# A hybrid decoder layer: sums of squares as two rounded products, and three engines' orders rewritten in the mixer loop

## The chip, the cores and the metric

The program runs on one core of one Trainium2 chip. The metric is the device time of one execution in microseconds (us); lower is better.

## The reference, cut to what matters

One decoder layer for 512 tokens of width 1024. The first half (the mixer) projects the normalised input onto eight heads of differential attention and eight groups of a Mamba-2 scan; the second half is a mixture of 32 experts, which the change leaves alone. What the change touches is the normalisation of queries and keys, and of the attention output:

```python
def _rms_norm(x, g, eps):
    xf = x.astype(jnp.float32)
    y = xf * lax.rsqrt(jnp.mean(xf * xf, axis=-1, keepdims=True) + eps)
    return (y * g.astype(jnp.float32)).astype(x.dtype)
...
    q = _rms_norm(q.reshape(b, s, ATTN_HEADS, 2, ATTN_HEAD_DIM), q_g, RMS_EPS) * (ATTN_HEAD_DIM ** -0.5)
    k = _rms_norm(k.reshape(b, s, ATTN_HEADS, 2, ATTN_HEAD_DIM), k_g, RMS_EPS)
...
    o = _rms_norm(o, sub_g, RMS_EPS) * (1.0 - lambda_init)
```

Around it in the same step of the kernel run the scan (decay, `mix`, state, `y`), the softmax of the scores, and the projections of the next step.

## The kernel before

The mixer is a loop of eight steps, one per attention head and scan group (`steps_of_mixer`; the eighth is written out after the loop). Every engine has a body of its own, and the order of the calls in it is the order of its instructions. The engines meet only at semaphores: `x_ready.at(i, n)` is the n-th signal of step i.

All projections use a split: a float32 matrix is rounded to fp32r (`hi`), the rest is kept as `lo`, and three products hi*hi, hi*lo, lo*hi stand for one float32 product. ScalarE (ACT) rounds a 512 KB weight piece in its `split(i, p)`, VectorE (DVE) subtracts in its own `split(i, p)`, and SyncE (SP) loads the next piece when VectorE is done. A step has nine pieces: 0 to 5 for projections 0 to 5 (`project(i, n)`), 6 to 8 for `project_vz`. Those of step i+1, 0 to 5, are split during step i.

TensorE (PE) goes through a step like this: `project(i, 4)` (queries), `turn_xb(0)` and `cb(0)`, `project(i, 5)` (keys), `turn_xb(1)`, `sum_squares(0)`, `y_and_state(0)`, `turn_xb(2)`, `project_vz(0)`, `sum_squares(1)`, `turn_xb(3)`, `cb(1)`, `project_vz(1)`, `scores(0)`, `y_and_state(1)`, and then, between quarters and halves of the next step's projections 0 to 3, three more scores and states, four `turn_diff`, the product with the values (L1443), `turn_y`, and the sum of squares of the attention output (L1451, osum below). `sum_squares(n)` waits for ScalarE's `squares(n)`, and is one float32 matmul with a block matrix of ones:

```python
pe.matmul(s_b[n][:], block_ones, sq[:, n], start=True, stop=True).then_inc(sums_ready.sem, 1)
```

Its result goes to ScalarE's `root(n)` (Ln, then Exp), then to VectorE's `norm_qk(n)` (L1063), and `scores(0)` waits for both. The result of osum goes through a Ln and an Exp on ScalarE (L928, L929) to VectorE's scaling of the attention output (L1197), behind which stand `split(i+1, 5)` and, in the next step, `taps(i+1, 3)` (L991), ScalarE's `silu(3)`, its table load, `make_decay(0)` (L822), `squares(0)` (L792, L793), `take_xb(0)` (L817), and the splits of pieces 7 and 8 (L711).

`y_and_state(1)` on TensorE waits for `make_mix(1)` of VectorE and for `make_xs(1)` of GpSimd (POOL). GpSimd has two jobs: `make_seg(u)` (L648, L651: two 128x512 operations on cumulative sums that SP brings by a DMA of its own) and `make_xs(u)` (L662 twice, L665: three 128x256 operations). Its order is seg 0, seg 1, xs 0, seg 2, xs 1, seg 3, xs 2, xs 3. SP brings the rows of seg 2 behind weight piece 2 and those of seg 3 behind piece 3, and such a piece waits for VectorE's split of the piece three before it:

```python
sp.wait_ge(plo_ready.sem, plo_ready.at(i + 1, p - MRAW + 1))
```

So the rows of seg 2 wait for VectorE's `split(i, 8)` (L985, `vz_lo`), those of seg 3 for its `split(i+1, 0)`.

VectorE's gated output (`gate_y(0)`, L1136) starts ScalarE's `norm_y(0)` (L845), behind which stands ScalarE's `split(i+1, 1)`, and behind that VectorE's. The logits are made at L1082, their negated maximum at L1087, and the difference of the softmaxes at L1100 to L1103.

Of the kernel before, what the change touches and what calls it, by code (L numbers as in the profile page):

```python
# [16 lines left out]
P = 128  # L17
D = 1024
# [214 lines left out]
def decoder_layer(nc, x, small, consts, onehot_rows, gffn, rel_bias, par, w_mix, w_dt, w_tail, w_rt, w1, w2, b12,  # L233
                  tok_ids, pads, out):
    with ExitStack() as ctx:
# [3 lines left out]
        def sem(name):  # L239
            return ctx.enter_context(nc.semaphore(name))  # L240
# [86 lines left out]
        def parts(name, shape, base, at):  # L327
# [12 lines left out]
        seg_of = (aux[:, 3 * T:4 * T].rearrange("p (k n) -> p k n", k=2), dT[:, 2:4, 0:2 * P])  # L340
        wm_hi = [parts(f"wm_hi{n}", [P, KT, P], base, at) for n, (base, at) in enumerate(spots)]
# [69 lines left out]
        ovhot_ready, ovhot_used, ovtable_ready, over_ready = (sem("ovhot_ready"), sem("ovhot_used"),  # L411
                                                              sem("ovtable_ready"), sem("over_ready"))

# [122 lines left out]
        with nc.Block() as block:  # L536
# [96 lines left out]
            @block.gpsimd  # L633
            def _(pool):
                prime(pool, seg_ready, xs_ready, gidx_ready, sidx_ready, pickb_ready, picks_ready, *spare_used[0:2])
                pool.wait_ge(decays_ready, 3)
                with pool.Fori(0, HEADS) as i:
                    h4 = i * HPG

                    def heads(table, u):  # L640
                        return table[:, u, bass.ds(h4, HPG)]

                    def make_seg(u):

                        pool.wait_ge(rows_in[u % 2].sem, rows_in[u % 2].at(i, u // 2 + 1))
                        of = seg_of[u % 2].rearrange("p k (h c) -> p k h c", h=2)
                        at = heads(a_all, u).rearrange("p (k h) -> p k h", k=2)
                        pool.tensor_tensor(of, of, at.unsqueeze(3).to_broadcast([P, 2, 2, P]), ALU.subtract).then_inc(  # L648
                            seg_ready.sem, 1)
                        pool.wait_ge(seg_ready.sem, seg_ready.at(i, 2 * u + 1))  # L650
                        pool.tensor_tensor(of, of, tri.unsqueeze(1).unsqueeze(1).to_broadcast([P, 2, 2, P]), ALU.mult).then_inc(  # L651
                            seg_ready.sem, 1)

                    def make_xs(u):

                        pool.wait_ge(m0_read.sem, m0_read.at(i, u + 1))
                        pool.wait_ge(m1_ready.sem, m1_ready.at(i, min(2 * u, 6)))
                        pool.wait_ge(ydiag_ready.sem, ydiag_ready.at(i, u))
                        pool.wait_ge(y_read.sem, y_read.at(i, u))
                        xv = xb[:, u, 0:GW].rearrange("p (h c) -> p h c", h=HPG)  # L660
                        for dst, src in ((xdt, heads(dtv, u)), (xw, heads(wend, u))):
                            pool.tensor_tensor(dst.rearrange("p (h c) -> p h c", h=HPG), xv,  # L662
                                               bcast_inner(src, HD), ALU.mult)
                        dsk = SMALL["d_skip"][0]
                        pool.tensor_tensor(xd.rearrange("p (h c) -> p h c", h=HPG), xv,  # L665
                                           bcast_inner(smalls[:, bass.ds(h4 + dsk, HPG)], HD),
                                           ALU.mult).then_inc(xs_ready.sem, 1)

                    make_seg(0)
                    for u in range(NT):  # L670
                        if u < NT - 1:
                            make_seg(u + 1)
                        make_xs(u)

            @block.scalar
            def _(act):
                prime(act, sigz_ready, phi_ready, ghi_ready, sigm_ready, mhi_ready, taps_ready, silu_ready, proj_read, root_ready, m0_read, decay_ready, exp_ready, yn_ready,
# [102 lines left out]
                def body(i, more):  # L780
# [99 lines left out]
                    make_decay(1)  # L880
# [21 lines left out]
                    softmax_exp(3)  # L902
                    norm_y(2, 0)
                    if more:
                        tap(i + 1, 1)
                        take_y(0, 7)
                        split(i + 1, 4)
                    else:
                        take_y(0, 7)
# [27 lines left out]
            def _(dve):  # L937
# [116 lines left out]
                def body(i, more):  # L1054
# [83 lines left out]
                    taps(i, 3)  # L1138
                    split(i, 6)
                    masked_cb(0)  # L1140
# [67 lines left out]
            def _(pe):  # L1208
# [115 lines left out]
                def body(i, more):  # L1324
                    def project_vz(t):
                        free_proj(i, 6 + t)
                        pe.wait_ge(plo_ready.sem, plo_ready.at(i, PIECES))
                        hi, lo = (w[:].rearrange("p (a b) -> p a b", a=KT) for w in (vz_hi, vz_lo))
                        for k in range(KT):
# [4 lines left out]
                        ins.then_inc(proj_done.sem, 1)  # L1334
# [340 lines left out]
            def _(pe):  # L1675
# [427 lines left out]
                def head_ov():  # L2103
                    pe.wait_ge(part_ready, NADD)
                    pe.wait_ge(first_added.sem, first_added.at(2))
                    for t in range(NT):
                        pe.wait_ge(ovhot_ready, t + 1)
# [3 lines left out]
                        ins.then_inc(ovhot_used if t < NT - 1 else ovtable_ready, 1)  # L2111
# [234 lines left out]
            def _(dve):  # L2346
# [369 lines left out]
                def head_ov():  # L2716
# [37 lines left out]
                    for t in range(NT):  # L2754
                        n = slice(TOPK * t, TOPK * (t + 1))
                        if t:
                            dve.wait_ge(ovhot_used, t)
# [4 lines left out]
                            ovhot_ready, 1)  # L2762
# [263 lines left out]
```

## Time and profile before

| | us |
|---|---|
| median of 3 runs | 1873.24 (1871.5 to 1873.26) |
| the profiled execution, its own time | 1872.48 |
| span of the profiled execution | 1870.4 |
| TensorE busy | 1831.9 |
| VectorE, ScalarE, GpSimd busy | 1128.1, 943.0, 359.9 |

The mixer loop runs from about 50 us to 590 us of the span, a step in 68.7 us. A row of the timeline has its start and its duration in us, engine, line, operation, output and inputs with shapes, and how many instructions were merged into it (x2, x3); in brackets stands the idle time of the engine before it, and what ended it. A float32 matmul is recorded as two rows of its line; the start of the next operation shows how long the engine was taken. Durations of matmuls overlap: in a stream, the distance of the starts is the price.

### The profile page before, as it was taken

The page shows a single profiled execution, that of the slowest core. Times are in us where ns is not written, and L with a number is a line of the kernel's source. Part 1 is how long each engine was busy: PE and PEld are TensorE (multiplying, and loading weights), DVE is VectorE, ACT ScalarE, POOL GpSimd, SP SyncE. Part 2 cuts the span into 40 slices and gives each one's busy share as a digit, 9 for nine tenths or more (in the row PEclk, how much of TensorE's full clock was granted, in tenths as well). Part 3 has the DMA queues.
Part 4 walks back from the last instruction along what each step waited for, and adds up shares of the span by engine and source line. Part 5 has one row for each costly group of instructions (what it writes and reads, how often), then busy time and mean ns, then how long its engine had stood idle before and what let it go on. Part 6 is the DMA issues. An engine that isn't in the chain of part 4 may idle for free.

```text
span 1870.4 us, 27360 instructions
## 1 busy us (share of the span) xinstructions
PE 1831.9 (98%) x8657; PEld 1298.2 (69%) x8657; DVE 1128.1 (60%) x1371; ACT 943.0 (50%) x1312; POOL 359.9 (19%) x401
## 2 busy tenths in 40 slices
PE   8999999999999999999999999999999999999998
PEld 6887887887888888887655665566556655665563
DVE  7767867867867333448654565456545654565456
ACT  5676676666667222325454455445544554455441
POOL 1322332332330000013111112111211121112010
PEclk9999999999999999999999999999999999999999
DMA  6232232232241222458999999999999999999998
GB/s 203 86 123 93 82 132 93 76 129 101 81 138 57 93 99 97 154 196 323 418 419 421 422 422 421 422 421 421 421 421 421 421 421 422 421 422 420 422 419 347
DMA packets 95377, 520.06 MB, mean 278 GB/s; under 512 B 13522, under 2 KB 20858, under 8 KB 45032
## 3 DMA queue, kind: packets, MB, share of 16 engines
q1 hardware_dynamic: 87672, 501.08, 67.3%
q0 software_dynamic: 6944, 16.30, 2.3%
q10 hardware_dynamic: 720, 2.16, 0.3%
q8 instruction: 22, 0.36, 0.1%
q14 instruction: 19, 0.16, 0.0%
HBM read 511.52 MB, written 25.51 MB: 287 GB/s over the span
## 4 chain that ended last, share of the span: by engine, by line
PE 81%; DMA 11%; DVE 4%; issue 2%; ACT 1%; SPq 0%; DVEq 0%; ACTq 0%
PE bank L1929 18%; PE bank L1301 15%; PE bank L1687 10%; DMA big<-in_w 10%; PE bank L1960 7%; PE bank L1331 7%; PE bank L1969 6%; PE bank L1952 2%; DVE w_lo L2535 2%; PE bank L1376 2%; PE bank L1359 1%; PE bank L1872 1%; DVE x_lo L2547 1%; PE bank L1443 1%; DMA keep<-in_b 1%
## 5 line engine op out<-in xcount | busy, mean ns | idle before, releaser
L2535 DVE TENSOR_TENSOR w_lo<-big,w_hi 128x2048 fp32r<-128x2048 f32 x141 | 321.7, 2291 | 205.3 <-ACT w_hi L2222 205.3
L2222 ACT ACTIVATE w_hi<-big 128x2048 fp32r<-128x2048 f32 x141 | 268.8, 1918 | 230.7 <-DMA big<-in_w 206.5
L1960 PE MATMUL bank<-big,keep 128*64 128x512 f32 x896 | 203.3, 598 | 0.0
L2535 DVE TENSOR_TENSOR w_lo<-keep,w_hi 128x2048 fp32r<-128x2048 f32 x48 | 109.9, 2292 | 103.4 <-ACT w_hi L2222 102.8
L1301 PE MATMUL bank<-h_hi,wm_hi 128*128 128x512 f32 x408 | 168.6, 413 | 0.0
L1301 PE MATMUL bank<-h_hi,wm_lo 128*128 128x512 f32 x408 | 159.5, 391 | 0.0
L1301 PE MATMUL bank<-h_lo,wm_hi 128*128 128x512 f32 x408 | 159.1, 390 | 0.0
L2222 ACT ACTIVATE w_hi<-keep 128x2048 fp32r<-128x2048 f32 x48 | 92.2, 1921 | 105.7 <-DMA keep<-in_w 96.1
L1960 PEld LDWEIGHTS bank<-big,keep 128*64 128x64 f32 x896 | 59.9, 136 | 117.3 <-issue 117.2
L1929 PE MATMUL bank<-w_hi,x_hi 128*128 128x512 f32 x480 | 134.4, 402 | 3.7 <-DVE w_lo L2535 3.7
L1929 PE MATMUL bank<-w_lo,x_hi 128*128 128x512 f32 x480 | 128.9, 390 | 0.0
L1929 PE MATMUL bank<-w_hi,x_lo 128*128 128x512 f32 x480 | 128.7, 390 | 0.0
L1929 PEld LDWEIGHTS bank<-w_hi,x_hi 128*128 128x128 f32 x480 | 86.6, 188 | 50.6 <-issue 21.8
L2356 DVE TENSOR_TENSOR g_lo<-keep,g_hi 128x1024 fp32r<-128x1024 f32 x35 | 42.9, 1225 | 113.0 <-ACT g_hi L2147 113.0
L1929 PEld LDWEIGHTS bank<-w_lo,x_hi 128*128 128x128 f32 x480 | 90.1, 188 | 19.6
L1929 PEld LDWEIGHTS bank<-w_hi,x_lo 128*128 128x128 f32 x480 | 90.1, 188 | 19.3
L1952 PE MATMUL bank<-w_hi,a_hi 128*128 128x512 f32 x256 | 84.5, 411 | 19.1 <-DVE w_lo L2535 19.1
L1301 PEld LDWEIGHTS bank<-h_hi,wm_hi 128*128 128x128 f32 x408 | 76.7, 188 | 26.2 <-issue 12.3
L991 DVE SCALAR_TENSOR_TENSOR big<-bank,par_sb,big 128x511 f32<-128x511 f32 (+2 forms) x96 | 71.8, 748 | 29.4 <-ACT big L732 20.7
L1331 PE MATMUL bank<-vz_hi,h_hi 128*128 128x384 f32 x256 | 89.2, 348 | 0.0
L1301 PEld LDWEIGHTS bank<-h_hi,wm_lo 128*128 128x128 f32 x408 | 76.6, 188 | 16.5
L1301 PEld LDWEIGHTS bank<-h_lo,wm_hi 128*128 128x128 f32 x408 | 76.8, 188 | 15.9 <-issue 1.9
(401 smaller groups left out, 3628.3 us busy)
## 6 DMA issues: line engine op xcount, KB each, us to landing
big<-in_w SPq DMA_DIRECT2D x290, 1024.0 KB, 13.4
keep<-in_w SPq DMA_DIRECT2D x94, 1024.0 KB, 14.1
big<-in_w_mix SPq DMA_DIRECT2D x72, 512.0 KB, 3.3
keep<-in_w_tail SPq DMA_DIRECT2D x44, 512.0 KB, 3.3
keep<-in_x SPq DMA_DIRECT2D x8, 512.0 KB, 4.8
aux<-acum_rows SPq DMA_DIRECT2D x16, 256.0 KB, 3.8
big<-acum_rows SPq DMA_DIRECT2D x16, 256.0 KB, 3.6
keep<-y_tok SPq DMA_DIRECT2D x4, 1024.0 KB, 13.2
```

The costliest lines, as they stand in the source:

```text
L991: ins = dve.scalar_tensor_tensor(out=conv[:, n, s:T], in0=proj_b[n % 2][:, 0:T - s], scalar=w, in1=conv[:, n, s:T], op0=ALU.mult, op1=ALU.add)
L1301: ins = pe.matmul(to[:], w[:, k], h[:, k], start=(k == 0 and w is hi and h is h_hi), stop=(k == KT - 1 and w is lo))
L1331: ins = pe.matmul(proj_b[t % 2][:, 0:VZ], h[:, k, t * P:(t + 1) * P], w[:, k], start=(k == 0 and h is h_hi and w is hi), stop=(k == KT - 1 ...
L1376: ins = pe.matmul(y_b[:, h * HD:(h + 1) * HD], mix[:, h], xdt[:, h * HD:(h + 1) * HD], start=True, stop=True)
L1687: ins = pe.matmul(bank[to][:], w[:, k], v[:, (x or 0) + k], start=(start and k == 0 and w is hi and v is x_hi_), stop=(stop and k == KT - ...
L1929: ins = pe.matmul(bank[c][:], x_part, w_part[:, s, c * 512:(c + 1) * 512], start=False, stop=n == KT - 1 and w_part is w_hi and x_part is lo)
L1952: ins = pe.matmul(bank[4 + c][:], a_part, w_part[:, s, o:o + 512], start=False, stop=k == KT - 1 and w_part is w_hi and a_part is lo)
L1960: ins = pe.matmul(bank[2 * (c // 2)][r, :], x_s[:, n % 4, CS * (n // 4):CS * (n // 4 + 1)], raw[s][:, c * 512:(c + 1) * 512], start=False, ...
L1969: ins = pe.matmul(bank[4][CS * c:CS * (c + 1), :], a_s[:, k % 4, CS * (k // 4):CS * (k // 4 + 1)], raw[s][:, o:o + 512], start=False, stop ...
L2222: act.activation(w_hi[:, s], raw[r], ACT.Copy).then_inc(hi_ready, 1)
L2356: dve.tensor_tensor(lo, of, hi.bitcast(F32), ALU.subtract).then_inc(glo_ready.sem, 1)
L2535: dve.tensor_tensor(w_lo[:, s], raw[r], w_hi[:, s].bitcast(F32), ALU.subtract).then_inc(lo_ready, 1)
```

## The change

- `sum_squares(n)` and osum are no longer one float32 matmul but two fp32r matmuls into one bank: ones times `sq_hi`, ones times `sq_lo`. The ones are rounded once before the loop (two copies on GpSimd).
- ScalarE gets three copies 128x512 a step (`high_square(0)`, `high_square(1)`, and one for osum), which round `sq` to `sq_hi`; GpSimd gets three subtractions 128x512 (`low_square`), which make `sq_lo`. TensorE waits for them. On GpSimd two stand between `make_xs(0)` and `make_seg(2)`, the third at the step's end; `make_seg` of the next step's first block moves ahead of the third.
- TensorE: `project_vz(0)` is cut in three. A quarter goes ahead of `y_and_state(0)`; `sum_squares(0)` moves behind five eighths of it. Each part waits only for the pieces that it reads. osum moves a quarter of `project(i+1, 3)` later.
- VectorE: `masked_cb(0)` ahead of `split(i, 6)`; `next_state(0)` and `sum_y(0)` ahead of `norm_qk(0)`; `split(i+1, 0)` behind `masked_cb(1)` and `make_mix(1)`; `norm_qk(1)` ahead of `silu_z(0)`.
- ScalarE: `silu(3)` and the table load ahead of `split(i, 6)`; `make_decay(1)` ahead of `root(0)`; `take_y(0, 7)` ahead of `norm_y(2, 0)`.
- Two semaphores of a later stage are shared with older ones; no instruction goes with it.

```diff
 (GpSimd)
+                def low_square(i, n, at):
+                    pool.wait_ge(sqhi_ready.sem, sqhi_ready.at(i, at))
+                    pool.tensor_tensor(sq_lo[:, n], sq[:, n], sq_hi[:, n].bitcast(F32), ALU.subtract).then_inc(
+                        sqlo_ready.sem, 1)
+                def body(i, more):
+                    make_seg(i, 1)
+                    make_xs(i, 0)
+                    low_square(i, 0, 1)
+                    low_square(i, 1, 2)
+                    make_seg(i, 2)
+                    make_xs(i, 1)
+                    make_seg(i, 3)
+                    make_xs(i, 2)
+                    make_xs(i, 3)
+                    if more:
+                        make_seg(i + 1, 0)
+                    low_square(i, 0, 3)
 (ScalarE)
+                    def high_square(n):
+                        act.wait_ge(proj_read.sem, proj_read.at(i, n + 1))
+                        act.wait_ge(diff_ready.sem, diff_ready.at(i, 0))
+                        act.activation(sq_hi[:, n], sq[:, n], ACT.Copy).then_inc(sqhi_ready.sem, 1)
                     silu(2)
-                    split(i, 6)
                     silu(3)
                     act.preload_act_table_set("natural_log_exp_and_others")
+                    split(i, 6)
                     make_decay(0)
                     squares(0)
                     take_xb(0)
+                    high_square(0)
                     split(i, 7)
                     split(i, 8)
                     squares(1)
                     take_xb(1)
+                    high_square(1)
                     take_xb(2)
+                    make_decay(1)
                     root(0)
-                    make_decay(1)
                     split(i + 1, 0)
...
                     act.activation(sq[:, 0], m1_b[:], ACT.Square).then_inc(osq_ready.sem, 1)
+                    act.wait_ge(osq_ready.sem, osq_ready.at(i, 1))
+                    act.activation(sq_hi[:, 0], sq[:, 0], ACT.Copy).then_inc(sqhi_ready.sem, 1)
 (VectorE)
                     taps(i, 3)
+                    masked_cb(0)
                     split(i, 6)
-                    masked_cb(0)
                     make_mix(0)
                     split(i, 7)
                     split(i, 8)
-                    norm_qk(0)
                     next_state(0)
                     sum_y(0)
-                    split(i + 1, 0)
+                    norm_qk(0)
                     masked_cb(1)
                     make_mix(1)
+                    split(i + 1, 0)
+                    norm_qk(1)
                     silu_z(0)
-                    norm_qk(1)
                     gate_y(0)
                     logits(0)
 (TensorE)
-                        pe.matmul(s_b[n][:], block_ones, sq[:, n], start=True, stop=True).then_inc(sums_ready.sem, 1)
+                        pe.wait_ge(sqlo_ready.sem, sqlo_ready.at(i, n + 1))
+                        pe.matmul(s_b[n][:], block_r[:], sq_hi[:, n], start=True, stop=False)
+                        pe.matmul(s_b[n][:], block_r[:], sq_lo[:, n], start=False, stop=True).then_inc(
+                            sums_ready.sem, 1)
...
                     turn_xb(1)
-                    sum_squares(0)
+                    project_vz(0, 0, KT // 4)
                     y_and_state(0)
                     turn_xb(2)
-                    project_vz(0)
+                    project_vz(0, KT // 4, 5 * KT // 8)
+                    sum_squares(0)
+                    project_vz(0, 5 * KT // 8, KT)
                     sum_squares(1)
...
                     turn_y(2, 8)
+                    project(i + 1, 3, KT // 2, 3 * KT // 4)
                     pe.wait_ge(osq_ready.sem, osq_ready.at(i, 1))
                     pe.wait_ge(logits_ready.sem, logits_ready.at(i, 4))
-                    pe.matmul(s_b[0][:], ones, sq[:, 0], start=True, stop=True).then_inc(osum_ready.sem, 1)
-                    project(i + 1, 3, KT // 2, KT)
+                    pe.wait_ge(sqlo_ready.sem, sqlo_ready.at(i, 3))
+                    pe.matmul(s_b[0][:], ones_r[:].to_broadcast([P, P]), sq_hi[:, 0], start=True, stop=False)
+                    pe.matmul(s_b[0][:], ones_r[:].to_broadcast([P, P]), sq_lo[:, 0], start=False, stop=True).then_inc(
+                        osum_ready.sem, 1)
+                    project(i + 1, 3, 3 * KT // 4, KT)
```

## Rows read from the trace of the kernel before

**Rows 1.** The page's busy line of TensorE.

```profile
PE 1831.9 (98%) x8657; PEld 1298.2 (69%) x8657; DVE 1128.1 (60%) x1371; ACT 943.0 (50%) x1312; POOL 359.9 (19%) x401
```

**Rows 2.** Waits of TensorE, 30 to 640 us: total, times, longest.

```profile
PEld bank L1301 <- issue: 14.2, 32, 0.8
...
PEld bank L1393 <- ACT keep L860: 1.6, 7, 0.2
```

**Rows 3.** Timeline of TensorE, third step of the mixer.

```profile
190.79 1.02 PE L1349 MATMUL bank<-keep,cst 128*128 128x512 f32 x2
...
197.50 1.02 PE L1349 MATMUL bank<-keep,cst 128*128 128x512 f32 x2
198.36 0.49 PE L1341 MATMUL bank<-cst,big 128*128 128x128 f32 x3
...
203.19 0.49 PE L1359 MATMUL bank<-big 64*128 64x128 f32 x4
203.61 1.10 PE L1376 MATMUL bank<-keep 128*128 128x64 f32 x8
...
214.96 0.92 PE L1359 MATMUL bank<-big 64*128 64x384 f32 x4
...
223.67 0.49 PE L1393 MATMUL bank<-cst,aux 128*128 128x128 f32 x3
...
243.79 1.02 PE L1451 MATMUL bank<-keep,cst 128*128 128x512 f32 x2
...
244.88 0.39 PE L1301 MATMUL bank<-h_lo,wm_hi 128*128 128x512 f32 x1
245.11 0.39 PE L1301 MATMUL bank<-h_hi,wm_lo 128*128 128x512 f32 x1
```

**Rows 4.** The same engine, `scores(0)` one step on.

```profile
271.86 0.49 PE L1359 MATMUL bank<-big 64*128 64x128 f32 x4
```

**Rows 5.** Timeline of GpSimd, third step.

```profile
189.49 1.60 POOL L665 TENSOR_TENSOR keep<-big,smalls 128x256 f32<-128x256 f32 x1
197.00 1.96 POOL L648 TENSOR_TENSOR aux<-aux,a_all 128x512 f32<-128x512 f32 x1 [5.91 <-DMA aux<-acum_rows]
...
202.07 1.06 POOL L665 TENSOR_TENSOR keep<-big,smalls 128x256 f32<-128x256 f32 x1
...
204.39 1.28 POOL L651 TENSOR_TENSOR big<-big,cst 128x512 f32<-128x512 f32 x1
```

**Rows 6.** Timeline of VectorE, third step.

```profile
180.23 2.54 DVE L991 SCALAR_TENSOR_TENSOR big<-bank,par_sb,big 128x511 f32<-128x511 f32 x3 [0.65 <-ACT big L732]
...
188.95 3.22 DVE L985 TENSOR_TENSOR vz_lo<-big,vz_hi 128x1024 fp32r<-128x1024 f32 x2 [1.76 <-ACT vz_hi L711]
...
202.58 0.83 DVE L1136 TENSOR_TENSOR big<-big 128x256 f32<-128x256 f32 x1
...
204.87 0.83 DVE L1087 TENSOR_SCALAR st<-st 128x2 f32<-128x2 f32 x1
206.12 1.23 DVE L985 TENSOR_TENSOR wm_lo<-big,wm_hi 128x1024 fp32r<-128x1024 f32 x1 [0.42 <-ACT wm_hi L718]
...
213.44 0.74 DVE L1082 TENSOR_TENSOR aux<-bank,biasT 128x256 f32<-128x256 f32 x2
...
222.56 0.62 DVE L1103 SCALAR_TENSOR_TENSOR aux<-aux,st 128x384 f32<-128x384 f32 x1
```

**Rows 7.** Timeline of ScalarE, third step.

```profile
186.37 0.58 ACT L792 ACTIVATE big<-bank 128x512 f32<-128x512 f32 x1
...
187.85 2.01 ACT L711 ACTIVATE vz_hi<-big 128x1024 fp32r<-128x1024 f32 x2
...
193.89 0.68 ACT L797 ACTIVATE keep<-bank,eps 128x512 f32<-128x512 f32 x1
...
203.53 0.42 ACT L845 ACTIVATE yn<-big 128x256 f32<-128x256 f32 x1 [2.40 <-DVE big L1136]
```

**Rows 8.** Timeline of the DMA queue: the rows of seg 2 are issued.

```profile
192.96 0.33 SPq L597 DMA_DIRECT2D aux<-acum_rows  x1
```

More of the change, by code:

```diff
@@ L340, in decoder_layer @@
         seg_of = (aux[:, 3 * T:4 * T].rearrange("p (k n) -> p k n", k=2), dT[:, 2:4, 0:2 * P])
+        block_r, ones_r = parts("block_r", [P, P], big_base, loop_mem.at + 4 * D), sb("ones_r", [P, 1], F32R)
+        sq_hi, sq_lo = parts("sq_hi", [P, 2, T], aux_base, 0), parts("sq_lo", [P, 2, T], keep_base, 23552 - 3 * KT * P)
         wm_hi = [parts(f"wm_hi{n}", [P, KT, P], base, at) for n, (base, at) in enumerate(spots)]
@@ L410, in decoder_layer @@
                                                            sem("halves_ready"))
-        ovhot_ready, ovhot_used, ovtable_ready, over_ready = (sem("ovhot_ready"), sem("ovhot_used"),
+        ovhot_ready, ovhot_used, ovtable_ready, over_ready = (Again(hot_ready, NT), Again(hot_used, NT - 1),
                                                               sem("ovtable_ready"), sem("over_ready"))
+        sqhi_ready, sqlo_ready = sig("sqhi_ready", 3), sig("sqlo_ready", 3)
         raw_in = [sem(f"raw_in{n}") for n in range(RAW)]
@@ L634, in _ @@
             def _(pool):
-                prime(pool, seg_ready, xs_ready, gidx_ready, sidx_ready, pickb_ready, picks_ready, *spare_used[0:2])
+                prime(pool, seg_ready, sqlo_ready, xs_ready, gidx_ready, sidx_ready, pickb_ready, picks_ready, *spare_used[0:2])
                 pool.wait_ge(decays_ready, 3)
[L637 to L673, printed above, removed]
@@ new lines, in heads, with make_seg @@
+                def heads(table, i, u):
+                    return table[:, u, bass.ds(i * HPG, HPG)]
+                def make_seg(i, u):
+                    pool.wait_ge(rows_in[u % 2].sem, rows_in[u % 2].at(i, u // 2 + 1))
+                    of = seg_of[u % 2].rearrange("p k (h c) -> p k h c", h=2)
+                    at = heads(a_all, i, u).rearrange("p (k h) -> p k h", k=2)
+                    pool.tensor_tensor(of, of, at.unsqueeze(3).to_broadcast([P, 2, 2, P]), ALU.subtract).then_inc(
+                        seg_ready.sem, 1)
+                    pool.wait_ge(seg_ready.sem, seg_ready.at(i, 2 * u + 1))
+                    pool.tensor_tensor(of, of, tri.unsqueeze(1).unsqueeze(1).to_broadcast([P, 2, 2, P]), ALU.mult).then_inc(
+                        seg_ready.sem, 1)
@@ new lines, in make_xs @@
+                def make_xs(i, u):
+                    pool.wait_ge(m0_read.sem, m0_read.at(i, u + 1))
+                    pool.wait_ge(m1_ready.sem, m1_ready.at(i, min(2 * u, 6)))
+                    pool.wait_ge(ydiag_ready.sem, ydiag_ready.at(i, u))
+                    pool.wait_ge(y_read.sem, y_read.at(i, u))
+                    xv = xb[:, u, 0:GW].rearrange("p (h c) -> p h c", h=HPG)
+                    for dst, src in ((xdt, heads(dtv, i, u)), (xw, heads(wend, i, u))):
+                        pool.tensor_tensor(dst.rearrange("p (h c) -> p h c", h=HPG), xv,
+                                           bcast_inner(src, HD), ALU.mult)
+                    dsk = SMALL["d_skip"][0]
+                    pool.tensor_tensor(xd.rearrange("p (h c) -> p h c", h=HPG), xv,
+                                       bcast_inner(smalls[:, bass.ds(i * HPG + dsk, HPG)], HD),
+                                       ALU.mult).then_inc(xs_ready.sem, 1)
@@ L675, in _ @@
+                make_seg(0, 0)
+                pool.tensor_copy(block_r[:], block_ones)
+                pool.tensor_copy(ones_r[:], ones[:, 0:1])
+                steps_of_mixer(pool, body)
             @block.scalar
             def _(act):
-                prime(act, sigz_ready, phi_ready, ghi_ready, sigm_ready, mhi_ready, taps_ready, silu_ready, proj_read, root_ready, m0_read, decay_ready, exp_ready, yn_ready,
+                prime(act, sigz_ready, sqhi_ready, phi_ready, ghi_ready, sigm_ready, mhi_ready, taps_ready, silu_ready, proj_read, root_ready, m0_read, decay_ready, exp_ready, yn_ready,
@@ L902, in body @@
                     softmax_exp(3)
+                    take_y(0, 7)
                     norm_y(2, 0)
@@ L1324, in body, with project_vz @@
                 def body(i, more):
-                    def project_vz(t):
-                        free_proj(i, 6 + t)
-                        pe.wait_ge(plo_ready.sem, plo_ready.at(i, PIECES))
+                    def project_vz(t, k0=0, k1=KT):
+                        if k0 == 0:
+                            free_proj(i, 6 + t)
+                        pe.wait_ge(plo_ready.sem, plo_ready.at(i, 6 + -(-k1 * VZ // D)))
                         hi, lo = (w[:].rearrange("p (a b) -> p a b", a=KT) for w in (vz_hi, vz_lo))
-                        for k in range(KT):
+                        for k in range(k0, k1):
                             for h, w in ((h_hi, hi), (h_hi, lo), (h_lo, hi)):
@@ L1333, in project_vz @@
                                                 stop=(k == KT - 1 and h is h_lo))
-                        ins.then_inc(proj_done.sem, 1)
+                        if k1 == KT:
+                            ins.then_inc(proj_done.sem, 1)
                     def turn_xb(u):
@@ L2106, in head_ov @@
                     for t in range(NT):
-                        pe.wait_ge(ovhot_ready, t + 1)
+                        pe.wait_ge(ovhot_ready.sem, ovhot_ready.at(t + 1))
                         for k in range(TOPK):
@@ L2756, in head_ov @@
                         if t:
-                            dve.wait_ge(ovhot_used, t)
+                            dve.wait_ge(ovhot_used.sem, ovhot_used.at(t))
                         dve.tensor_tensor(ov_hot, bcast_mid(slot_no, TOPK), bcast_inner(posx[:, n], CAP), ALU.is_equal)
@@ L2761, in head_ov @@
                         dve.tensor_tensor(ovid_hot, ovid_hot, bcast_inner(entry1[:, n], NOV + 1), ALU.mult).then_inc(
-                            ovhot_ready, 1)
+                            ovhot_ready.sem, 1)
                     dve.wait_ge(ovtable_ready, 1)
```

4 lines of the change are left out of this document (1 added, 3 removed).

## The prediction

> **What bounds the kernel now.** I read the page first, then TensorE's waits over the mixer, then one step of the mixer on each engine's timeline, then the DMA queue. TensorE is busy for 98% of the span [rows 1]. Over 30 to 640 us its list of waits names no engine or DMA of any weight: what there is are issue gaps, 14.2 us at most in one group, and 1.6 us for the wait of turn_diff(3) on ScalarE's take_y [rows 2]. So TensorE sets the step. scores(0) starts at 203.19 us and 68.67 us later again [rows 3, 4]; this is the period P. Two things follow. Work taken from TensorE is worth its time, as long as no wait opens; and since today's waits are all just met, what counts is by how much: how long before TensorE came was each operand ready? Those margins are what the change spends. All clock times below are those of the third step.
>
> **What is removed.** A float32 sum of squares takes TensorE from 197.50 to 198.36, so 0.86 us [rows 3]. Two fp32r matmuls at the spacing of the projections, 244.88 to 245.11, so 0.23 us each [rows 3], take 0.46. Three per step: 3 x 0.40 = 1.2 us. Cutting project_vz(0) adds one more change between float32 and fp32r matmuls: nothing at one end, and at the other the 0.86 again that osum and its changeover share (243.79 to 244.88 is 1.09, that is 0.86 + 0.23 [rows 3]); I take 0.1. The earlier silu(3) and take_y end small gaps, 0.2 us for take_y [rows 2]. Net about 1.1 us a step; over eight steps 8.8 us. This is the whole gain there can be: with no new wait the span falls from 1870.4 to about 1861.6, time about 1864.
>
> **What is added, and where it lies.** A copy 128x512 on ScalarE costs 0.58 us by its nearest row, a 128x512 read of PSUM [rows 7], about 0.5 in a queue. low_square on GpSimd is not in the trace; nearest are its own 128x512 operations, 1.28 for L651 [rows 5]; I take 1.1, bounds 1.0 and 1.3. Neither engine is full, so busy time is no matter. What matters is the chain in which they stand.
>
> Chain A, from osum to the rows of seg 2. osum ran at 243.79, which is 175.12 one period earlier. It now comes six matmuls later, 6 x 0.23 = 1.4 us, and takes 0.4 less: its root is 1.0 us later. VectorE had 0.65 us of idle ahead of taps(3) at 180.23 [rows 6], so taps(3) and silu(3) come about 0.4 later. Putting silu(3) ahead of split 6 does not shorten ScalarE's sum up to make_decay(0), so squares(0) is 0.4 later, and high_square(0) adds 0.5 ahead of split 7: 187.85 becomes 188.7 [rows 7]. VectorE's splits 7 and 8 then ask at 189.8 and 191 instead of 188.95.
>
> Here the row to read is GpSimd's L665: 1.60 us at 189.49, 1.06 at 202.07, while two splits on VectorE took 3.22 us beside it, where a split alone takes 1.23; and the 128x2 operation L1087 took 0.83 us, to 205.70, just past the end of GpSimd's L651, 204.39 + 1.28 = 205.67 [rows 5, 6]. An operation on one of the two engines waits out the one on the other, and where both have work they take turns. The Trainium skill (SBUF — State Buffer, "Who interferes with whom") says that a VectorE instruction with two SBUF inputs and a GpSimd instruction that reads SBUF block each other for a whole instruction; the trace agrees, by the 1.60 and the 0.83 us. Without turns every operation would take its short time, GpSimd's make_xs(1) would be over near 201.6, and the sum would be the full gain, 1864; with them it is what follows.
>
> Taking turns, split 7 runs 189.9 to 191.0, GpSimd's L665 to 191.6, split 8 to 192.6. It ended at 192.17 before [rows 6]. SP issued the rows of seg 2 at 192.96, 0.8 behind it, and GpSimd began at 197.00, 4.0 behind that [rows 5, 8]; now 193.4 and 197.5. low_square(0) and (1) lie in GpSimd's 5.91 us of idle before that [rows 5] and are done by 192.7 to 195: hidden, and in time for the sums (below).
>
> Chain B, queries and keys. sum_squares(0) moves from 190.79 to about 194.9: turn_xb and a quarter of vz, y_and_state(0), turn_xb(2), nine matmuls of vz. Its root starts on ScalarE at 195.5 instead of 193.89 [rows 7]; root(1) stays where it was, near 199.5. So norm_qk(0) and split(i+1, 0) reach VectorE 1.1 to 1.7 us later. next_state(0) and sum_y(0), moved forward, fill 0.8 us of the hole, but masked_cb(1), make_mix(1), split(i+1, 0), norm_qk(1), silu_z(0) and gate_y(0) now all stand behind 198.1, and beside GpSimd's make_seg(2) and make_xs(1) from 197.5 on. The uncontested prices are estimates from the rows. VectorE: a split of 1024 elements 1.23 [rows 6], 0.1 of it under the next start, so 1.1; 512 elements about 0.6, 256 about 0.35. GpSimd: L651 1.28 and L648 a little less, for 512 elements; 256 elements half of that, 0.6 [rows 5]. Turn by turn: L648 to 198.6, mix to 199.2, L651 to 200.4, split to 201.5, L662 to 202.0, norm_qk(1) to 202.7, L662 to 203.2, silu_z to 203.5, L665 to 204.0, gate_y to 204.4.
>
> Before, L665 of make_xs(1) ended at 203.13 and TensorE took it at 203.61: 0.4 us of margin; gate_y(0) ended at 203.41 [rows 3, 5, 6]. Now TensorE, 0.9 us ahead by then, gets norm_qk(1) at 202.75 and make_xs(1) at about 204.1: it waits over 1 us and is 0.1 to 0.5 later than before. If GpSimd wins the first turn the two ends swap by 0.4, not more.
>
> What is late next: gate_y(0) at 204.4 is 1.0 later. ScalarE's norm_y(0) was waiting for it, idle 2.40 us [rows 7], and VectorE's split(i+1, 1) at 206.12 waits behind it [rows 6]: now 207.1. There it meets make_seg(3), whose rows are asked for behind split(i+1, 0), now at 202.2, there at 206.2. Before, seg 3 was over at 205.67 [rows 5]. A turn costs VectorE another 0 to 1.1 us. From there VectorE's queue has no idle of weight up to the softmax difference at 222.56, and its margins to TensorE are small: logits(1) ended at 214.18, scores(2) started at 214.96, 0.7; the difference ended at 223.18, its transposition started at 223.67, 0.4 [rows 3, 6]. With VectorE 1.0 to 2.1 us late, turn_diff(2) is 0.6 to 1.7 us late. That is by how much the period grows, since nothing after it gives time back: the rest of the step is TensorE's own, and osum of this step starts chain A of the next.
>
> Osum itself: the copy, then low_square, both behind ScalarE's Square, are ready near 244.3, and TensorE comes at 245.2; hidden, 0.9 us of cover. make_seg(i+1, 1) waits behind it on GpSimd, 3 us later than today; it is wanted by make_decay(1), past 193 in the next step.
>
> **The sum.** Per step +0.6 to +1.7, I take +1.0, nearer the lower end because each turn may fall the short way. Eight passes, the first without an osum before it: 7.5 x 1.0 = 7.5 us. Span 1870.4 + 7.5 = 1877.9; the profiled execution's own time was 2.1 above its span, and the median 0.8 above that time: 1880.8, say 1881.
>
> **The rivals.**
> - R1, the full gain: no new wait, 1864 (with half of the wait at y_and_state(1), 1868). For it: TensorE's list of waits is empty today, GpSimd is 19% busy. Against it: the 0.4 us of margin at 203.61 and the turns. It decides if make_xs(1) ends before 202.6, that is if its operations and VectorE's do not add up.
> - R2, only make_xs(1) binds: the period moves by -0.3 to +0.4, VectorE recovers before 223. Time 1871 to 1876. For it: VectorE had 0.42 us idle before 206.12. Against it: no more than that.
> - R3, deeper: seg 3 costs the full turn in each step, also on later operations, +1.7 a step: 1886.
> - R4, low_square for osum is not ready at 245.2, because GpSimd is held up by make_seg(i+1, 0): then TensorE loses up to 2 us a step, 1889. The rows of that segment were there long before, so it is unlikely.
>
> **How the numbers follow.** The forecast's own case (+0.5 to +1.5 a step, 1877 to 1885) has 0.45, R1 0.26, R2 0.18, R3 and R4 together 0.11. The range from 1864 to 1886 takes in R1's full gain at its lower end and R3 at its upper. A measurement here can tell about 0.2%, 3.7 us. Faster by more: R1 and a little of R2, 0.28. Within it: most of R2 and the edge of my own case, 0.17. Slower: 0.55. The likeliest case's own range is 1877 to 1885.
>
> **What would show it.** The sum of squares as two rows 0.23 us apart: the gain is there. TensorE's waits, empty today, would name GpSimd (L665, make_xs) before L1376 and VectorE before L1359 and L1393. L665 of make_xs(1) would end at a later point after osum than today, gate_y(0) about 1 us later, and VectorE's 128x2 and 128x256 operations near the new seg 3 would be longer. The period would read 69 to 70 us. If it reads 67.5, the turns do not bind and I am wrong at chain B; if TensorE waits before osum, I am wrong on the cover there.

## The result, and the profile after

The changed kernel takes 1885.70 us (median of 4 runs, 1884.53 to 1887.28), the kernel before 1872.37 us in the same comparison: a ratio of 1.0072, 95% interval 1.0055 to 1.0090. It is 13.3 us slower. The profiled execution took 1885.89 us with a span of 1884.1 us.

The page's busy line, which answers to [rows 1]: TensorE is busy for 1.2 us less, in a span that is 13.7 us longer.

```profile
PE 1830.7 (97%) x8657; PEld 1301.9 (69%) x8657; DVE 1133.1 (60%) x1371; ACT 956.3 (51%) x1336; POOL 402.7 (21%) x427
```

TensorE's waits from 30 to 650 us. The list of before named no engine among its matmuls [rows 2]. Now GpSimd is the first and VectorE the next three; L1410 is in `y_and_state`, L1393 in `scores`, L1402 in `cb`. The last row is from the waits of TensorE's weight loads, which the others leave out; L1427 is in `turn_diff`.

```profile
PE bank L1410 <- POOL keep L666: 6.6, 8, 0.8
PE bank L1393 <- DVE big L1092: 4.1, 8, 0.9
PE bank L1393 <- DVE aux L1111: 1.5, 4, 0.4
PE bank L1402 <- DVE keep L1145: 1.3, 4, 0.8
PE bank L1479 <- issue: 0.8, 1, 0.8
...
PEld bank L1427 <- DVE aux L1132: 1.4, 5, 0.3
```

TensorE's timeline in the third step, answering to [rows 3]; in brackets its idle time and what ended it. The step's anchor is the start of `turn_y(2, 8)` (first row here; 174.69 in the trace before), so 3.05 us are to be taken off for comparison. The last row is `scores(0)` of the next step [rows 4].

```profile
177.74 0.38 PE L1435 MATMUL bank<-cst,keep 128*128 128x128 f32 x2
...
179.57 0.39 PE L1489 MATMUL bank<-sq_hi,ones_r 128*128 128x512 f32 x1
179.80 0.40 PE L1490 MATMUL bank<-sq_lo,ones_r 128*128 128x512 f32 x1
...
197.77 0.39 PE L1381 MATMUL bank<-sq_hi,block_r 128*128 128x512 f32 x1
198.00 0.39 PE L1382 MATMUL bank<-sq_lo,block_r 128*128 128x512 f32 x1
...
205.75 0.49 PE L1393 MATMUL bank<-big 64*128 64x128 f32 x4 [0.63 <-DVE big L1092]
207.07 1.08 PE L1410 MATMUL bank<-keep 128*128 128x64 f32 x8 [0.82 <-POOL keep L666]
...
219.13 0.92 PE L1393 MATMUL bank<-big 64*128 64x384 f32 x4 [0.40 <-DVE aux L1111]
...
228.13 0.55 PE L1427 MATMUL bank<-cst,aux 128*128 128x128 f32 x3
...
275.54 0.49 PE L1393 MATMUL bank<-big 64*128 64x128 f32 x4 [0.25 <-DVE big L1092]
```

The reader is to see two things. The products do what they were made for: `sq_lo` starts 0.23 us behind `sq_hi`. And from wait to wait TensorE falls back. Less 3.05, `scores(0)` is at 202.70 (before 203.19, 0.5 early), `y_and_state(1)` at 204.02 (203.61, 0.4 late), `scores(2)` at 216.08 (214.96, 1.1 late), `turn_diff(2)` at 225.08 (223.67, 1.4 late). Over the eight starts of `scores(0)`, 64.92 to 556.38 us, a period is 70.21 us on average; before it was 68.64 (65.82 to 546.30).

GpSimd and VectorE in the same step, answering to [rows 5, 6]:

```profile
194.29 3.53 POOL L673 TENSOR_TENSOR sq_lo<-keep,sq_hi 128x512 fp32r<-128x512 f32 x2
200.86 1.04 POOL L649 TENSOR_TENSOR aux<-aux,a_all 128x512 f32<-128x512 f32 x1 [3.04 <-DMA aux<-acum_rows]
201.98 1.62 POOL L652 TENSOR_TENSOR aux<-aux,cst 128x512 f32<-128x512 f32 x1
203.56 1.59 POOL L663 TENSOR_TENSOR keep<-big,dtv 128x256 f32<-128x256 f32 x1
...
206.13 0.79 POOL L666 TENSOR_TENSOR keep<-big,smalls 128x256 f32<-128x256 f32 x1
209.20 1.04 POOL L649 TENSOR_TENSOR big<-big,a_all 128x512 f32<-128x512 f32 x1 [2.28 <-DMA big<-acum_rows]
210.32 2.17 POOL L652 TENSOR_TENSOR big<-big,cst 128x512 f32<-128x512 f32 x1
```

```profile
183.55 2.52 DVE L1020 SCALAR_TENSOR_TENSOR big<-bank,par_sb,big 128x511 f32<-128x511 f32 x3
...
192.63 2.79 DVE L1014 TENSOR_TENSOR vz_lo<-big,vz_hi 128x1024 fp32r<-128x1024 f32 x2 [1.66 <-ACT vz_hi L731]
...
202.37 2.31 DVE L1014 TENSOR_TENSOR wm_lo<-big,wm_hi 128x1024 fp32r<-128x1024 f32 x1
204.60 1.10 DVE L1092 SCALAR_TENSOR_TENSOR big<-big,smalls,keep 128x512 f32<-128x512 f32 x1
...
206.49 0.72 DVE L1165 TENSOR_TENSOR big<-big 128x256 f32<-128x256 f32 x1
...
209.91 1.41 DVE L1014 TENSOR_TENSOR wm_lo<-big,wm_hi 128x1024 fp32r<-128x1024 f32 x1 [1.65 <-ACT wm_hi L738]
...
211.43 1.08 DVE L1130 TENSOR_TENSOR st<-st,eps 128x1 f32<-128x1 f32 x1
...
227.45 0.62 DVE L1132 SCALAR_TENSOR_TENSOR aux<-aux,st 128x384 f32<-128x384 f32 x1
```

Read them against each other. GpSimd's L652, 1.28 us alone, takes 1.62; an L663 takes 1.59 for 0.6 of work because VectorE's split is running; the split takes 2.31 because it first waited for L652. A VectorE operation on one number per partition, 0.16 us before, takes 1.08: it waits out L652 of seg 3, the one that took 2.17. It does so in every step: 1.05 to 1.08 us in seven of the eight, 0.80 in the last. The last row is the difference of the softmaxes that `turn_diff(2)` takes; with the 3.05 us taken off it ends at 225.02, 1.84 us later than before.

### The profile page after: what moved, and what is told of

It reads as the page before. It is cut to its first block, busy times and chain, and to the rows that moved or that the text cites. A ratio compares the mean times of both kernels' runs of the same rounds, so it can differ in the third digit from the quotient of the medians.

```text
span 1884.1 us, 27471 instructions
## 1 busy us (share of the span) xinstructions
PE 1830.7 (97%) x8657; PEld 1301.9 (69%) x8657; DVE 1133.1 (60%) x1371; ACT 956.3 (51%) x1336; POOL 402.7 (21%) x427
## 4 chain that ended last, share of the span: by engine, by line
PE 70%; DMA 10%; DVE 10%; issue 5%; ACT 3%; POOL 1%; DVEq 0%; ACTq 0%; SPq 0%; POOLq 0%
PE bank L1969 18%; PE bank L1330 11%; PE bank L1727 10%; DMA big<-in_w 9%; PE bank L2000 7%; PE bank L2009 6%; PE bank L1361 3%; PE bank L1992 2%; PE bank L1774 2%; DVE w_lo L2575 2%; DVE wm_lo L1014 1%; PE bank L1410 1%; PE bank L1912 1%; DVE x_lo L2587 1%; PE bank L1479 1%
## 5 line engine op out<-in xcount | busy, mean ns | idle before, releaser
L1361 PE MATMUL bank<-vz_lo,h_hi 128*128 128x384 f32 x256 | 86.6, 338 | 0.0
## 6 DMA issues: line engine op xcount, KB each, us to landing
big<-in_w SPq DMA_DIRECT2D x290, 1024.0 KB, 13.7
```

## The experiments

Each was measured beside the kernel before on the same chip, and the ratio is to that. The groups of experiments ran on different chips, on which the kernel before took 1872.2 to 1873.3 us, so differences between experiments of under about 1 us say nothing. "After" is the changed kernel.

**Rows a piece earlier** (`a_rows_early`).

```diff
-SEG_AFTER = (2, 3, 5, 6)
+SEG_AFTER = (1, 2, 5, 6)
```

> The changed kernel, but the DMA queue brings the rows of seg 2 behind weight piece 1 and those of seg 3 behind piece 2 (one piece earlier each). My theory (VectorE and GpSimd take turns, make_seg(2), make_xs(1) and make_seg(3) come too late and collide with VectorE's queue): make_seg(2) starts about 1.6 us earlier in the step, seg 3 right behind make_xs(1); TensorE's waits before y_and_state(1), scores(2) and turn_diff(2) shrink to 0.3 us or less, the period falls from 70.2 to between 68.3 and 69.2 us, time 1869 to 1878. Rival A (the extra work itself, three copies and three subtractions, makes the engines too slow): 1885, unchanged. Rival B (chain B alone, the late root(0), binds at scores(0)): the wait before scores(0) of 0.6 to 0.9 us stays and the time falls by 3 us at most, to 1883.

Measured: 1874.54 us, 1.0009 of before (1.0000 to 1.0019); period 68.61. What is left of TensorE's waits, then GpSimd and VectorE in its third step (here the anchor is near that of before):

```profile
PE bank L1393 <- DVE aux L1111: 2.8, 7, 0.4
PE bank L1402 <- DVE keep L1145: 2.3, 8, 0.6
```

```profile
195.75 1.04 POOL L649 TENSOR_TENSOR aux<-aux,a_all 128x512 f32<-128x512 f32 x1 [1.27 <-DMA aux<-acum_rows]
...
206.26 1.23 DVE L1014 TENSOR_TENSOR wm_lo<-big,wm_hi 128x1024 fp32r<-128x1024 f32 x1 [1.54 <-ACT wm_hi L738]
```

No work was taken away, two transfers were issued earlier, and 11 us of the 13 are gone. The waits for GpSimd and for `norm_qk` have left the list. The wait at `scores(2)` did not shrink to 0.3 us as I had expected: it is 0.4 us, in seven steps instead of four. That the extra work is too much for the engines (rival A) and that the late root alone binds (rival B) are both out. What is left is VectorE's queue, which stands idle for 1.54 us ahead of its `split(i+1, 1)` and is late afterwards.

**The same on the kernel before** (`b_rows_early`).

> Control: the kernel before with the same two row loads one piece earlier. TensorE had no wait there, so by my theory nothing changes: 1872, within 1 us. By the rival that earlier rows are worth something by themselves (GpSimd done earlier, fewer turns) up to 3 us faster.

Measured: 1872.59 us, 0.9994 (0.9984 to 1.0004). Nothing. The early rows repair what the change broke; they are worth nothing by themselves.

**Only seg 3's rows earlier** (`a_seg3_early`).

```diff
-SEG_AFTER = (2, 3, 5, 6)
+SEG_AFTER = (2, 2, 5, 6)
...
-                        if p in SEG_AFTER:
-                            u = SEG_AFTER.index(p)
+                        for u in [n for n, q in enumerate(SEG_AFTER) if q == p]:
```

> The changed kernel, with only the rows of seg 3 earlier (behind piece 2, after those of seg 2). My theory splits in two here: the wait before y_and_state(1) (0.8 us) stays, since make_seg(2) is as late as before; the collision of VectorE's split(i+1, 1) and softmax difference with make_seg(3) goes, so that turn_diff(2) is only 0.6 us late instead of 1.5. Period about 69.3, time 1877 to 1880. If the late gate_y(0) alone makes VectorE late and the collision is nothing, 1885; if the collision is all, 1873.

Measured: 1880.68 us, 1.0036 (1.0022 to 1.0050), its runs spread from 1873.11 to 1885.07; period 69.26. Its list still names GpSimd at `y_and_state` (6.6 us in 8 waits, as after) and `norm_qk` (3.5 us), and no longer the logits, the state or `cb`. The collision is gone: the operation on one number per partition takes 0.16 us in all eight steps. The time is 0.7 us above what I had expected, 1877 to 1880.

How much is seg 3 and how much seg 2 can't be read from this median, because the ten executions follow TensorE's granted clock: 1873.11 and 1874.72 us at 1.000, 1877.54 (the profiled one) at 0.998, and 1879.44 to 1885.07 at 0.995 to 0.997. In the profiled one the clock fell to its 1.2 GHz level for some 3 us twice, right behind the waits for `norm_qk` and GpSimd; these two periods are 70.53 and 70.24 us, the five others 68.81 on average. The periods of after without such a dip average 70.04. So at the full clock the collision with seg 3 costs 1.2 us a step. What the best version below mends besides costs another 1.2 (68.81 against its 67.58), about as much as the saving. The two dips of the clock cost 1.6 us each.

**No low parts** (`a_no_low`).

```diff
-                    pool.tensor_tensor(sq_lo[:, n], sq[:, n], sq_hi[:, n].bitcast(F32), ALU.subtract).then_inc(
-                        sqlo_ready.sem, 1)
+                    pool.sem_inc(sqlo_ready.sem, 1)
...
-                        pe.matmul(s_b[n][:], block_r[:], sq_lo[:, n], start=False, stop=True).then_inc(
+                        pe.matmul(s_b[n][:], block_r[:], sq_hi[:, n], start=False, stop=True).then_inc(
```

> The changed kernel without GpSimd's three subtractions: the low parts are left out and the high product is taken twice, so that TensorE's work is the same and the sums are not the reference's. My theory: two of the subtractions lay in GpSimd's idle time ahead of seg 2 and the third in that behind seg 0, so the time stays at 1884 to 1886. Rival (GpSimd's added work binds): it falls by 4 us or more, below 1882.

Measured: 1886.39 us, 1.0069 (1.0053 to 1.0086). That is 0.4 us above the expected 1884 to 1886, and the same as after. GpSimd's 24 subtractions cost nothing that can be measured: they do lie in its idle time.

**The new orders with the old sums** (`a_f32`).

```diff
-                        pe.wait_ge(sqlo_ready.sem, sqlo_ready.at(i, n + 1))
-                        pe.matmul(s_b[n][:], block_r[:], sq_hi[:, n], start=True, stop=False)
-                        pe.matmul(s_b[n][:], block_r[:], sq_lo[:, n], start=False, stop=True).then_inc(
-                            sums_ready.sem, 1)
+                        pe.matmul(s_b[n][:], block_ones, sq[:, n], start=True, stop=True).then_inc(sums_ready.sem, 1)
...
-                    high_square(0)
-                    high_square(1)
...
-                    low_square(i, 0, 1)
-                    low_square(i, 1, 2)
```

and the same for osum.

> The changed kernel with its new orders and places, but with the float32 sums of squares of before: no copies to sq_hi, no subtractions. My theory: what costs is where the sums and the steps stand (root(0) 1.65 us later, osum 1.4 us later), so most of the loss stays although all the new work is gone: ScalarE is 0.5 us a step earlier at split 7, but osum's root is 0.4 us later and so is that of the queries. Time 1881 to 1888. Rival (the copies and subtractions cost the time): taking them away brings it back to 1873 to 1876.

Measured: 1892.23 us, 1.0103 (1.0086 to 1.0120); period 70.97. The new work gone, and the kernel is 6.5 us slower still, 4 us beyond the upper end that I had written. I had priced the later roots at 0.4 us and no more. The largest wait is now another one, `cb(2)` for `next_state(1)`, up to 1.3 us a step:

```profile
PE bank L1392 <- DVE keep L1138: 6.6, 7, 1.3
PE bank L1383 <- DVE aux L1104: 3.1, 8, 0.4
```

The loss sits in the places and orders; the products give back part of it. Which of the moved steps makes it, no run separates.

**Only osum as two products, on the kernel before** (`b_osum`). Of the change this has the copy behind `Square`, one `low_square`, GpSimd's new order at the step's end, and osum a quarter of the projection later:

```diff
+                    project(i + 1, 3, KT // 2, 3 * KT // 4)
                     pe.wait_ge(osq_ready.sem, osq_ready.at(i, 1))
...
-                    pe.matmul(s_b[0][:], ones, sq[:, 0], start=True, stop=True).then_inc(osum_ready.sem, 1)
-                    project(i + 1, 3, KT // 2, KT)
+                    pe.wait_ge(sqlo_ready.sem, sqlo_ready.at(i, 1))
+                    pe.matmul(s_b[0][:], ones_r[:].to_broadcast([P, P]), sq_hi[:, 0], start=True, stop=False)
+                    pe.matmul(s_b[0][:], ones_r[:].to_broadcast([P, P]), sq_lo[:, 0], start=False, stop=True).then_inc(
+                        osum_ready.sem, 1)
+                    project(i + 1, 3, 3 * KT // 4, KT)
```

> The kernel before, with only osum as two rounded products, a quarter of the projection later, with its copy and subtraction and GpSimd's new order at the end of a step. All else is of before. TensorE is spared 0.4 us a step. My theory: the saving is worth nothing as it stands, since TensorE then waits for silu(3) ahead of cb(0), which ends at 184.5 in the step shown and binds already: 1871 to 1874. The naive sum: 8 x 0.4 = 3.2 us faster, 1870 or below. The rival that the late osum alone makes the following step late: slower by 2 us or more.

Measured: 1871.99 us, 0.9997 (0.9987 to 1.0007); period 68.55 instead of 68.64. TensorE's timeline and ScalarE's in the fourth step:

```profile
252.82 0.48 PE L1387 MATMUL bank<-big 128*128 128x128 f32 x2 [0.19 <-ACT big L802]
```

```profile
252.08 0.61 ACT L802 ACTIVATE big<-big 128x512 f32<-128x512 f32 x1
```

`silu(3)` ends at 252.69, `cb(0)` starts at 252.82. Of 0.4 us saved 0.1 arrive. TensorE's list has this wait in six steps, 1.2 us in all.

**ScalarE's split ahead of `norm_y(0)`** (`a_split1`).

```diff
-                    norm_y(0, 0)
                     split(i + 1, 1)
+                    norm_y(0, 0)
```

> The changed kernel with ScalarE's split(i+1, 1) ahead of norm_y(0), in the 3.3 us in which ScalarE waits for gate_y(0). The rows of seg 2 and 3 stay late. My theory: TensorE's waits ahead of scores(0) and y_and_state(1) stay (0.6 to 0.9 and 0.8 us); those ahead of cb(2), scores(2) and turn_diff(2) shrink, since VectorE has its split 1 us earlier. Period about 69.2 to 69.7, time 1877 to 1882. Rival (VectorE's lateness comes from GpSimd's turns alone): unchanged, 1885.

Measured: 1877.79 us, 1.0030 (1.0019 to 1.0042); period 69.43. As expected the first two waits stay (5.8 us for GpSimd, 3.7 us for `norm_qk`) and what stands behind them shrinks to 0.4 us in all:

```profile
PE bank L1410 <- POOL keep L666: 5.8, 7, 0.8
PE bank L1393 <- DVE big L1092: 3.7, 8, 0.9
PE bank L1479 <- issue: 0.8, 1, 0.8
PE bank L1393 <- DVE aux L1111: 0.4, 1, 0.4
```

So VectorE's lateness came by two ways, GpSimd's turns and the chain `gate_y(0)`, `norm_y(0)`, `split(i+1, 1)`. This repair alone is worth 8 us, the earlier rows alone 11.

**The three repairs together** (`a_best`): both edits above, and in the eighth step `norm_y(2, 0)` ahead of `take_y(0, 7)`.

> The changed kernel with three repairs: rows of seg 2 and 3 one weight piece earlier, ScalarE's split(i+1, 1) ahead of norm_y(0), and in the last step norm_y(2) ahead of take_y as before. With the rows alone 1874.5 was measured, and TensorE still waited 0.3 and 0.4 us a step for VectorE ahead of cb(2) and scores(2), and 0.8 plus 1.2 us once ahead of the last value product. My theory: these waits go, the products' saving of about 1 us a step appears, period 67.5 to 67.9, time 1864 to 1868, faster than both kernels. If another wait takes their place, 1870 to 1874.

Measured: 1864.23 us (1863.19 to 1865.39), 0.9958 (0.9941 to 0.9975): 8 us faster than the kernel before, 21 us faster than the change. Period 67.58. TensorE's waits again name almost nothing, and VectorE's split comes right behind the logits, without the 1.65 us of idle:

```profile
PE bank L1395 <- DVE big L1094: 0.3, 1, 0.3
```

```profile
202.93 0.28 DVE L1118 TENSOR_SCALAR st<-st 128x2 f32<-128x2 f32 x1
203.12 1.21 DVE L1016 TENSOR_TENSOR wm_lo<-big,wm_hi 128x1024 fp32r<-128x1024 f32 x1
```

**The repairs on the kernel before** (`b_rows_split1`).

> Control: the kernel before with two of the three repairs, rows of seg 2 and 3 a piece earlier and ScalarE's split(i+1, 1) ahead of norm_y(0). It has no waits to remove. My theory: 1871 to 1873, unchanged, so the repairs are worth nothing without the products. Rival (the repairs are the whole gain of the best version): 1864 to 1867.

Measured: 1872.40 us, 0.9999 (0.9989 to 1.0009). Nothing again.

**The best version with float32 sums** (`best_f32`).

> The best version with the float32 sums of before in the new places: no copies, no subtractions. My theory: three matmuls of 0.86 instead of 0.46 us, so at least 1.2 us a step more than the best version if no wait opens: 1874 or more; up to 1880, since the roots come 0.4 us later and VectorE's margin is small. If the products are worth nothing it stays at 1864.

Measured: 1877.19 us, 1.0024 (1.0014 to 1.0034), period 69.22: 13.0 us more than with the products, 1.64 us a step, of which 3 x 0.4 are the matmuls themselves; the rest is not traced. So the gain of the best version is the products'; orders and repairs alone lose 4.4 us.

**The old order in the eighth step** (`a_last_order`).

```diff
+                    if more:
+                        take_y(0, 7)
+                        norm_y(2, 0)
...
+                    else:
+                        norm_y(2, 0)
+                        take_y(0, 7)
```

> The changed kernel with ScalarE's old order in the eighth step alone: norm_y(2) ahead of take_y(0). In the changed kernel TensorE waits 0.8 us and 1.2 us of weight loading once ahead of the last value product, because ScalarE's last take_diff(3) stands behind steps that now wait for turn_y. My theory: this wait goes, 1 to 2 us in all, time 1883 to 1885; everything else is as it was (period 70.2).

Measured: 1884.59 us, 1.0061 (1.0044 to 1.0077). The wait is gone: from `turn_diff(3)` (L1427, L1429) to the value product (L1479, L1481) it was 2.84 us after, and is 1.95 here. First the changed kernel, then this one:

```profile
590.78 0.60 PE L1427 MATMUL bank<-cst,aux 128*128 128x128 f32 x4
593.62 2.39 PE L1479 MATMUL bank<-big 128*128 128x512 f32 x8 [0.84 <-issue]
```

```profile
589.70 0.60 PE L1429 MATMUL bank<-cst,aux 128*128 128x128 f32 x4
591.65 2.39 PE L1481 MATMUL bank<-big 128*128 128x512 f32 x8
```

The 0.9 us are in the trace; in the times 1.1 us lie between the medians, less than the intervals can part.

**The copy behind the splits** (`a_copy_late`).

```diff
-                    high_square(0)
                     split(i, 7)
                     split(i, 8)
+                    high_square(0)
```

> The changed kernel with high_square(0) behind ScalarE's splits 7 and 8 instead of ahead of them, so that the 0.5 us of the copy leaves chain A. My theory: VectorE's splits and the rows of seg 2 come up to 0.5 us earlier, but make_seg(2) cannot begin before norm_qk(0) on VectorE is over, 0.3 us earlier than now; so a gain of 0 to 0.4 us a step, time 1882 to 1886. Rival (the copy ahead of the splits is what makes the step late): 1880 or less.

Measured: 1882.19 us, 1.0054 (1.0037 to 1.0071), period 69.79: 0.4 us a step, about 3.5 us in all. The intervals of this ratio and of that of after (1.0055 to 1.0090) overlap, so the gain is likely rather than shown. The trace agrees with it: at the full clock the periods are 69.68 against 70.04. It does not agree with one reason that I had written: GpSimd's make_seg(2) did not stay behind `norm_qk(0)`, it is recorded from 199.07, inside that operation (198.77 to 199.52), and took 1.35 us instead of 1.04. The copy in chain A costs something, at the upper end of what I expected, but is far from being the cause.

## Why the prediction was right

Direction and mechanism held, place by place. The size was taken too small: 1881 was forecast. The time, 1885.7, lies just outside the likeliest case's own 1877 to 1885, and only 0.3 us inside the range, whose upper end came from rival R3. That it still lies inside is luck of that number. The period, 70.2 us, is just above the 69 to 70 that I had named as the sign.

- **The saving.** 0.46 instead of 0.86 us per sum holds (0.23 us between the starts). That the whole possible gain was about 1.1 us a step holds too: the best version has a period of 67.58 against 68.64.
- **Chain A.** Less 3.05 us, VectorE's taps(3) starts at 180.50 (forecast 180.6: idle 0.65 spent, 0.4 later), splits 7 and 8 end at 192.4 (192.6), GpSimd's make_seg(2) starts at 197.8 (197.5). The rows landed 4.5 us after their issue at 196.20, and the trace names their transfer as what GpSimd waited for. `a_rows_early` shows that this is where the step is made late.
- **Chain B, turn by turn.** norm_qk(1) ends at 202.65 (202.7), make_xs(1) at 203.87 (204.0), gate_y(0) at 204.16 (204.4). TensorE waits 0.63 and 0.82 us there; forecast were 0.6 to 1.1. This is the part that a busy share cannot show: GpSimd is 21% busy, and TensorE waits 6.6 us for it.
- **What is late next.** split(i+1, 1) at 206.86 (207.1) and the collision with seg 3: 1.08 us for an operation of 0.16. scores(2) is 1.1 late, turn_diff(2) 1.4. Before `turn_diff` TensorE's matmuls have no wait in the list; it is its weight load that waits, 0.2 to 0.3 us.
- **The term that was mis-sized.** The turn at seg 3. The working had gate_y(0) 1.0 us late, then a turn of 0 to 1.1, less the 0.4 of margin: +0.6 to +1.7 a step. I took +1.0 "because each turn may fall the short way". In the third step gate_y(0) and split(i+1, 1) are 0.75 late and the softmax difference 1.84: the turn cost 1.1, its full size, and the operation that waits out L652 shows it in every step. No period is less than 1.1 longer than before; the average is +1.57, seven times, 11.0 us. So what came is R3's condition, seg 3 at the full turn in each step, and R3's number, 1886, is the measured one. It was no separate mechanism: my own terms reached +1.7 too, and I had cut my case off at +1.5.
- **What was not in it.** The tail. From the last `scores(0)` to the first product with the output weights (L1687 before, L1727 after) the trace before has 44.2 us and after 47.6, 3.4 more. About 1.5 are the same waits as in each step. 0.9 are the wait ahead of the last value product that `a_last_order` took away: I had counted the earlier take_y as a gain of 0.2 a step and not looked at the eighth step, where ScalarE has rounding of its own behind it. The rest, 1.0 us, is not traced to a cause. On the other side the first `scores(0)` is 0.9 us early. 11.0 + 3.4 - 0.9 = 13.5 us, of 13.7 by which the span grew; the other 0.2 lie behind that product. Nor did the prediction have the dips of the granted clock, which the last section prices.
- **Osum's cover** held: no wait stands ahead of L1489. low_square is 1.3 us by the last step's row, at the upper bound, and cost nothing (`a_no_low`).
- **The rivals.** R1, the full gain of 1864, did not come with this change; it came when its two late transfers, one late split and the order in the eighth step were mended. R2 fell: VectorE did not recover before `turn_diff(2)`. R4 fell.

By the Trainium skill (SBUF — State Buffer, "Who interferes with whom") an instruction of VectorE with two SBUF inputs and one of GpSimd that reads SBUF block each other for a whole instruction; the 1.59 us of an L663 beside the 2.31 us of a split agree with that here.

## What to carry to other kernels

When one engine sets the time and waits for nobody, write down for each of its waits how long before it the operand was there. A change that saves a microsecond a step is worth it only where these margins (here 0.4 to 0.7 us) are larger than what it moves. And look for what was queued behind a moved step on another engine, its transfers above all: here two DMAs issued one weight piece too late cost 11 us, while the added subtractions cost nothing and the one copy that was moved out of the chain gave back 3.5 us at most. If a chain of turns has been added up from rows, trust the sum, and don't shade it.

## What the runs showed of the hardware

The granted clock of TensorE, 1.00 throughout the mixer before, fell to its lower level, 1.2 GHz, for about 3 us in three of the eight steps after. Each dip begins within about 1.5 us of the start of `y_and_state(1)`, right behind TensorE's waits at `scores(0)` and there: 0.92 and 0.82 us in the second step, 0.71 and 0.83 in the sixth, 0.46 and 0.82 in the seventh. The waits alone don't decide it: two steps with 0.63 and 0.82 have no dip, and `a_f32`, with single waits of up to 1.3 us, has none at all. Here is the second step, with the busy time of each engine, the granted clock (of 2.4 GHz, so 0.5 is the 1.2 GHz level) and the DMA share:

```profile
132.00:135.00 3.00, 2.16 (x13) 1.84 (x11) 3.00 (x3) 1.05 (x3) 3.00 (x3) 1.00 0.00 0
135.00:138.00 3.00, 2.09 (x14) 1.84 (x15) 2.49 (x7) 1.25 (x5) 1.26 (x2) 0.89 0.79 262
138.00:141.00 3.00, 3.00 (x11) 2.73 (x10) 1.73 (x3) 2.94 (x9) 2.48 (x2) 0.54 0.00 0
141.00:144.00 3.00, 3.00 (x19) 2.87 (x17) 2.77 (x7) 2.10 (x4) 0.73 (x1) 1.00 0.50 175
```

The three periods with such a dip are 70.67, 70.56 and 70.07 us, the four without 70.16, 69.79, 69.99 and 70.22: 0.4 us more on average, so about 1 us of the 13, as far as seven periods can tell. A dip is cheap here because VectorE binds next: in the three steps with a dip, TensorE's later waits at `cb(2)` and `scores(2)` are missing. Where the collision with seg 3 is gone, in `a_seg3_early`, a dip costs 1.6 us, and the times of its executions spread over 12 us with the granted clock. `a_rows_early` and the best version, without the two waits, have no dip in the mixer.
